# Identity products into an unread bank at three still places of TensorE, in a two-layer hybrid kernel

## The reference, cut to what matters

```python
scores = sigmoid(h @ router_w)
biased = scores + router_b
grp = biased.reshape(..., 8, 4)
sel = argmax(top_k(grp, 2)[0].sum(-1))          # one group of each token
_, idx = top_k(where(in_group(sel), biased, -inf), 2)
w = scores[idx] / sum(scores[idx])
for e in range(32):
    y += combine[..., e] * ((silu(h @ w_gate[e]) * (h @ w_up[e])) @ w_down[e])
x = x + gate * y
```

## Time and profile before

| | |
|---|---|
| timed runs, median | 925.45 us (925.25 to 926.0, 3 runs) |
| span of the profiled execution | 922.1 us |
| TensorE (PE) busy | 836.3 us, 91% of the span |
| VectorE (DVE) busy | 399.9 us, 43% |
| mean granted TensorE clock | 0.968 |
| HBM traffic | 288.17 MB read, 8.91 MB written |

### The profile page before, as it was taken

The page is one execution under the profiler, slowest core; times in us unless marked ns, Lnnn a source line. Parts: engine busy times, 40 slices in busy tenths (PEclk is TensorE's granted clock), DMA queues, the critical chain, the costliest instruction groups (busy, mean ns, idle before and its releaser), DMA issues.

```text
span 922.1 us, 9986 instructions
## 1 busy us (share of the span) xinstructions
PE 836.3 (91%) x3715; PEld 372.5 (40%) x3715; DVE 399.9 (43%) x829; ACT 166.9 (18%) x413; POOL 156.9 (17%) x185
## 2 busy tenths in 40 slices
PE   4899999999899999977969999879897999978786
PEld 2444445446633333322338444536545333322222
DVE  1379998316233233313243687558635122212111
ACT  2301012206200000000023111537412000000000
POOL 2100193121202012211021231410220100000000
PEclk9999999999999999999989999989997999999998
DMA  9999355625698999999899558422375899999994
GB/s 364 406 419 403 140 202 245 273 92 183 224 411 341 385 421 423 423 423 423 353 420 427 199 194 355 182 92 92 125 332 184 359 425 423 422 425 428 424 423 176
DMA packets 27878, 291.87 MB, mean 317 GB/s; under 512 B 5030, under 2 KB 5336, under 8 KB 9132
## 3 DMA queue, kind: packets, MB, share of 16 engines
q1 hardware_dynamic: 23472, 283.25, 75.0%
q0 software_dynamic: 4272, 7.80, 2.4%
q10 hardware_dynamic: 76, 0.02, 0.0%
HBM read 288.17 MB, written 8.91 MB: 322 GB/s over the span
## 4 chain that ended last, share of the span: by engine, by line
PE 64%; DMA 17%; DVE 14%; ACT 2%; issue 2%; SPq 1%; POOL 0%; DVEq 0%; ACTq 0%; POOLq 0%
PE bank L1360 21%; DMA ring<-in_gu_pack 14%; DVE WORK L2364 10%; PE bank L1385 10%; PE bank L501 9%; PE bank L1520 5%; DMA ring<-in_win_pack 3%; PE bank L1226 3%; PE bank L1467 2%; PE bank L1303 2%; PE bank L1369 1%; PE bank L558 1%; PE bank L567 1%; PE bank L592 1%; PE bank L1135 1%
## 5 line engine op out<-in xcount | busy, mean ns | idle before, releaser
L1360 PE MATMUL bank<-ring,WORK 128*64 128x512 f32 x352 | 107.3, 627 | 11.4 <-DMA ring<-in_gu_pack 7.2
L1360 PE MATMUL bank<-ring,hT 128*64 128x512 f32 x368 | 112.2, 611 | 6.0 <-DMA ring<-in_gu_pack 3.7
L2364 DVE SCALAR_TENSOR_TENSOR WORK<-WORK,par 128x512 f32<-128x512 f32 x116 | 90.7, 860 | 0.0
L501 PE MATMUL bank<-ring,hT 128*128 128x512 f32 (+2 forms) x256 | 88.0, 499 | 0.7 <-ACT hT L1635 0.7
L1385 PE MATMUL bank<-ring,WORK 128*64 128x512 f32 x384 | 86.8, 595 | 0.6 <-ACT WORK L1677 0.6
L2254 DVE SCALAR_TENSOR_TENSOR WORK<-WORK,bank 128x256 f32<-128x256 f32 x16 | 7.7, 480 | 139.4 <-ACT WORK L1672 139.4
L2254 DVE SCALAR_TENSOR_TENSOR hT<-hT,WORK,bank 128x256 f32<-128x256 f32 x18 | 8.6, 480 | 135.4 <-ACT hT L1672 128.6
L1677 ACT ACTIVATE WORK<-bank 128x256 f32<-128x256 f32 x34 | 13.0, 383 | 265.5 <-PE bank L1369 265.5
L501 PEld LDWEIGHTS bank<-ring,hT 128*128 128x128 f32 x256 | 46.0, 190 | 35.8 <-issue 34.0
L1467 PE MATMUL bank<-hT,ring 128*128 128x512 f32 x128 | 57.4, 608 | 1.8 <-DMA ring<-in_win_pack 1.8
L1520 PE MATMUL bank<-ring,B 128*128 128x512 f32 x128 | 56.6, 596 | 0.8 <-DVE B L2381 0.8
(11 more groups left out here) (346 smaller groups left out, 1205.7 us busy)
## 6 DMA issues: line engine op xcount, KB each, us to landing
ring<-in_gu_pack SPq DMA_DIRECT2D x41, 2048.0 KB, 16.8
ring<-in_mod_pack SPq DMA_DIRECT2D x24, 2048.0 KB, 11.3
ring<-in_down_pack SPq DMA_DIRECT2D x21, 2048.0 KB, 26.4
WORK<-in_gu_pack SPq DMA_DIRECT2D x5, 2048.0 KB, 17.6
ring<-in_wout_pack SPq DMA_DIRECT2D x4, 2048.0 KB, 12.2
ring<-in_win_pack SPq DMA_DIRECT2D x3, 2048.0 KB, 37.0
X<-in_gu_pack SPq DMA_DIRECT2D x3, 2048.0 KB, 8.7
B<-in_gu_pack SPq DMA_DIRECT2D x3, 2048.0 KB, 23.8
```

The lines of the kernel that those rows point to most:

```text
L501: mm = pe.matmul(dst[:, 0:hi - lo], hT[:, k, t * P:(t + 1) * P], w[:, k, :], start=k == 0, stop=k == KC - 1)
L1360: mm = pe.matmul(dst[ST * x:ST * x + ST, :], HG[L][s][:, k, :], columns(units[x], 512 * k, 512), start=k == 0, stop=k == KC - 1)
L2364: ins = dve.scalar_tensor_tensor(out=acc, in0=src, scalar=w, in1=acc, op0=ALU.mult, op1=ALU.add)
```

## The change

`busy` is called at three more places. In layer 1's router it is called with 14 products right after the logits are turned, and with 5 right after the ranks, both into bank 6. Between the layers TensorE waits for `x_added` to be 10 and then multiplies 10 times into bank 1. Nothing reads the results.

```diff
@@ route(L)
                 turn_logits((3, 5)[L], 3, (nt - 2, nt - 1))
+                if L == 1:
+                    busy(6, 14)
 
                 H2 = h2_order(nt)
@@ route(L)
                 mm.then_inc(sem("ranks"), 1)
+                if L == 1:
+                    busy(6, 5)
                 if L == 0:
                     h_rows(range(4, 8))
@@ TensorE's list
             overflow_pe(pe, 0)
             spread_last()
+            pe.wait_ge(sem("x_added"), 10)
+            busy(1, 10)
 
             turn_pair("a1", 0, range(4))
             mod(7)
```

## The result

The kernel after takes 920.11 us (median of 8 runs, 919.13 to 921.5), the kernel before 924.9 us over its own 8 runs of the same comparison (920.33 to 926.0). The ratio of the runs is 0.9944, with a 95% interval of 0.993 to 0.9959: 5.2 us less (3.8 to 6.5). The two medians differ by 4.8 us. The forecast was 920.3.

What follows compares the result with a forecast made beforehand. The prediction took TensorE's half-clock router work, which restarts the idle weights' stream, to bound the end. Gains of 0.25 + 3.6 + 1.3 + 0 = 5.15 us from 925.45 gave 920.3 us, range 919.0 to 925.2.

Steps and rivals of the forecast that it cites:

- The likeliest case, clock held through the router: Layer 1's router: TensorE's clock stays at 1.00 from 697 to 719 us, total 920.3 us (919.4 to 921.2), chance 0.63.
- Price of an instruction: Added f32 products, two instructions each: 0.114 us per instruction at full clock, 0.22 as the upper end.
- both covers: Layer 1's router: TensorE's waits for VectorE hide the added 28 and 10 instructions (3.2 and 1.1 us) at no cost.
- L1303 at full clock: Gathering of the first expert's rows in layer 1: 7.09 us becomes 3.5, a gain of 3.6 us (3.4 to 3.7).
- First gate/up product: First expert of layer 1: the first 16 instructions take 3.5 us instead of 4.82, a gain of 1.3 us.
- Ranks: Rank product in layer 1's router: 1.46 us becomes about 0.85, but VectorE's own work limits the gain to 0.25 us.
- Between the layers: Block of 20 instructions before layer 1: clock stays up, but the modulation weights' wait takes the saving; 0 us gained.
- The end follows the stream's restart: From 720 us weights stream without pause, so a microsecond TensorE gains between 700 and 719 is one at the end.
- First rival, the clock falls all the same: Between the router blocks, before the gathering: only 0.25 us stays, 925.2 us, chance 0.15; held in part 921.5 to 924, 0.12.
- thin places: Layer 1's router: 699.8 to 700.3, the few-column rank products and about 0.6 us before the gathering, where the clock might fall.
- Second rival, the block meets a fallen clock: After the logits: block runs up to 6.2 us at half clock, ranks 2.5 us late, 927.95 us, chance 0.06.
- Third rival, the gain is given back to the DMA: Layer 1's weights' stream restarts no earlier despite TensorE's gain: 925.2 us, chance 0.04.

## Why the prediction was right

- *The likeliest case, clock held through the router*: right in mechanism and in place. The router blocks alone give it back whole in one of two comparisons. That the time agrees to 0.2 us, 920.3 against 920.11, is partly luck: the forecast started from 925.45 and took off 5.15; the kernel before had a median of 924.9 in the comparison, and the medians differ by 4.8.
- *Price of an instruction*: forecast 0.114 us, measured 0.113 over 48. The first block took 3.2 us of issue and ended before the ranks; both covers held, with 0.33 and 0.45 us to spare against the forecast's 0.4 and some 0.2.
- *L1303 at full clock*: forecast 3.5 us with bounds to 3.65, measured 3.79, so 3.30 us of gain and not 3.6. The term was slightly mis-sized. From its start to the next product's it is 706.98 - 703.26 = 3.72 us for 32 instructions, 0.116 each, so 64 columns did not lie between the rows of 2 and of 128 columns as the forecast had it. *First gate/up product*: 1.24 against 1.3. *Ranks*: 0.26, from what is left of the 4.80 after 3.30 and 1.24, against 0.25. The sum in the router is 4.80 against 5.15.
- *Between the layers*: forecast 0, measured 1.0004. The forecast's reason, that the wait for weights takes what the clock gives, fits the profiled execution of the full change (a wait of 1.90 us). It does not fit that of the block alone, where the wait was 0.43 us and the total was unchanged all the same, so the reason is not shown. The forecast also used two pairs of bounds for this term, -0.5 and +0.5 in its text and -0.3 and +0.6 in its sum; the result does not depend on it.
- *The end follows the stream's restart*: shown. 4.5 us of TensorE at the first product cost most of themselves, at the ninth nothing, and from the issue of the pair of loads to the end it was 201.8 to 203.0 us in every profiled execution. (The chain before turns to "DMA" at 786.28, 67 us behind that issue at 719.16, and not the forecast's 99.)
- *First rival, the clock falls all the same*: in none of the ten profiled executions with both blocks did the clock fall in the router. With the first block alone it is what happened, so the second block is what excludes it, as the forecast's "thin places" had it.
- *Second rival, the block meets a fallen clock*: not seen for the first block. The second block alone is the same case. There the gathering started 1.0 us later than before, counted from the transposes, and 4.1 us came back in the gathering and the product behind it, because the clock rose. The forecast's argument that a dense block lifts a fallen clock fits this, and my later expectation for the second block alone, which ignored it, was wrong. The rule of the Trainium skill on transposes, which would have made this rival likely, is contradicted for the f32 transposes of this kernel by their 3.79 us.
- *Third rival, the gain is given back to the DMA*: excluded. The load into X is issued at 707.14, 0.09 us behind the end of the gathering at 707.05, and the next pair and the end moved with it.

## What to carry to other kernels

Look for dense work that runs at half clock right behind a wait on another engine, and fill the wait with products nobody reads, to just under the engine's wait; price them from a row of the same shape. Fill every thin place of the stretch: covering only the first let the clock fall later, onto the next product, and gained nothing that the timed runs show; covering only the second gained 1.8 us of some 5. Then ask what the saved time reaches: it was worth its full size where TensorE restarted an idle stream of weights, and nothing that could be measured where loads were queued.

## What the runs showed of the hardware that was not expected

- After ten dense instructions at half clock (2.33 us) ahead of the narrow gathering the clock rose 1.3 us into it, while 7 us of the gathering alone left it at 0.50. That is one profiled execution of each.
- In the one pair of executions that shows it, a block of products ahead of TensorE's register loads cost more than itself: 3.7 us for 2.05 us of products.
- The total of one and the same kernel moves more between executions than the change is worth: the kernel before ran from 918.85 to 927.52 us in the 29 runs of one comparison. The clock falls at other places from one execution to the next (near 228 in the kernel after and not in the one before, near 254 in ten of the fourteen), and the router's transposes start anywhere from 690.42 to 695.67. The router's stretch, 17.56 to 17.58 us in seven profiled executions of the same router, was the sharper measure.
